# Down of the later groups as seven half-size products in a hybrid decoder step

## The reference, cut to what matters

```python
h = h + (ga * (oa @ w_oa) + gb * (ob @ w_ob)) @ w_out
hn = _rms_norm(h, norm_ffn)
h = h + (jax.nn.silu(hn @ w_gate) * (hn @ w_up)) @ w_down
...
y_prompt = _rms_norm(hp, norm_final)[:, N_META:]
```

## Time and profile before

| | |
|---|---|
| median of 3 runs | 3308.24 us (3306.07 to 3310.15) |
| profiled execution, its own time as the span from first to last instruction | 3313.0 us |
| TensorE busy | 3231.5 us, 98%, 23418 matmuls |
| VectorE, ScalarE, GpSimd busy | 1982.6, 1510.4, 431.1 us |
| moved | 392.45 MB, mean 118 GB/s |

### The profile page before, as it was taken

The page is one execution under the profiler, slowest core; times in us unless marked ns, Lnnn a source line. Parts: engine busy times, 40 slices in busy tenths (PEclk is TensorE's granted clock), DMA queues, the critical chain, the costliest instruction groups (busy, mean ns, idle before and its releaser), DMA issues. The chain is left out here.

```text
span 3313.0 us, 58927 instructions
## 1 busy us (share of the span) xinstructions
PE 3231.5 (98%) x23418; PEld 2825.3 (85%) x23418; DVE 1982.6 (60%) x3740; ACT 1510.4 (46%) x3156; POOL 431.1 (13%) x511
## 2 busy tenths in 40 slices
PE   8999999999999999999999999999999999999998
PEld 7877789999998777898998777889998777789896
DVE  6635545444547654685766754686575855578483
ACT  5434443222234554463554654455454654446362
POOL 2211200432503111000003021000001212000000
PEclk9889999999999999999999999999999999999999
DMA  4211013656643111354553211345463211246462
GB/s 161 65 41 66 28 58 115 230 188 208 248 153 110 54 52 58 119 161 134 170 190 110 73 41 51 110 141 163 140 211 126 75 50 46 77 133 183 124 179 96
DMA packets 142816, 392.45 MB, mean 118 GB/s; under 512 B 18289, under 2 KB 20289, under 8 KB 139073
## 3 DMA queue, kind: packets, MB, share of 16 engines
q1 hardware_dynamic: 142544, 388.69, 36.8%
HBM read 353.95 MB, written 35.69 MB: 118 GB/s over the span
## 5 line engine op out<-in xcount | busy, mean ns | idle before, releaser
L631 DVE TENSOR_TENSOR wl<-raw,wh 128x512 fp32r<-128x512 f32 (+1 forms) x795 | 750.6, 951 | 572.2 <-ACT wh L624 569.4
L624 ACT CAST wh<-raw 128x512 fp32r<-128x512 f32 (+1 forms) x795 | 635.7, 808 | 457.6 <-PE bank L902 374.7
L902 PE MATMUL bank<-xnT,wh 128*128 128x512 f32 (+2 forms) x2432 | 726.2, 382 | 7.3 <-ACT gate L1691 5.8
L902 PE MATMUL bank<-hnT,wh 128*128 128x256 f32 (+2 forms) x3016 | 580.7, 290 | 3.4 <-ACT V L1989 3.4
L902 PEld LDWEIGHTS bank<-xnT,wh 128*128 128x128 f32 x2432 | 430.4, 193 | 80.6 <-issue 16.5
L902 PEld LDWEIGHTS bank<-hnT,wh 128*128 128x128 f32 x3016 | 473.7, 188 | 9.0 <-ACT V L1989 4.2
L902 PE MATMUL bank<-hid,wh 128*128 128x512 f32 (+1 forms) x1760 | 467.5, 353 | 0.0
L902 PE MATMUL bank<-xnT,wl 128*128 128x512 f32 (+2 forms) x1280 | 461.7, 365 | 0.0
L902 PE MATMUL bank<-hnT,wl 128*128 128x256 f32 (+2 forms) x1508 | 437.2, 290 | 0.0
L902 PE MATMUL bank<-Tm,wh 128*128 128x256 f32 x2016 | 368.8, 282 | 0.2
L902 PEld LDWEIGHTS bank<-hid,wh 128*128 128x128 f32 x1760 | 309.5, 188 | 45.8
(11 more groups left out here) (382 smaller groups left out, 4488.3 us busy)
## 6 DMA issues: line engine op xcount, KB each, us to landing
raw<-in_wstream SPq DMA_DIRECT2D x346, 512.0 KB, 3.5
raw<-wsum SPq DMA_DIRECT2D x252, 256.0 KB, 3.4
raw<-in_wstream SPq DMA_DIRECT2D x189, 256.0 KB, 2.8
ops_in<-in_wstream SPq DMA_DIRECT2D x44, 512.0 KB, 7.6
wsum<-ops_out SPq DMA_DIRECT2D x22, 1024.0 KB, 6.3
hT<-in_xT SPq DMA_DIRECT2D x4, 2048.0 KB, 8.9
out_yp_out<-hT SPq DMA_DIRECT2D x16, 512.0 KB, 3.0
xr<-in_x_prompt SPq DMA_DIRECT2D x12, 512.0 KB, 7.2
```

Source lines behind the costliest of these rows:

```text
L624: act.copy(hi_cell(n), raw_cell(n)).then_inc(sem("hi_done"), 1)
L631: nc.vector.tensor_tensor(lo_cell(n), raw_cell(n), hi_cell(n).bitcast(F32), ALU.subtract).then_inc(sem("lo_done"), 1)
L902: ins = nc.tensor.matmul(*a, **k)
```

## The change

The FFN is worked in three chunks of 6, 8 and 8 columns in every group. In group 0 down stays plain, with one unit per output column, and GpSimd makes the four sums for 12 pairs of down's output columns beside the 22 of gate and up. In the later groups down is made of the same seven half-size products: for each pair of output columns (r) all seven, over 3 or 4 block pairs; the units are 384 or 512 columns wide. VectorE adds the banks to `hT` in between, and these adds take the place of copies. The operand sums of hid, their low parts, the sums of squares of down's output and the low parts of the next input are made by GpSimd. The next group's token rows and columns are loaded earlier, in parts, and the rows squared among the products of the last chunk.

```diff
-FFC, FFK = 2, DFF // P // 2
+NFF = DFF // P
+CHUNKS = ((0, 6), (6, 14), (14, NFF))
+DOWN_ORDER = [(r, op) for r in range(NPAIR) for op in OPS]
...
+            def seven_down(c):
+                j0, j1 = CHUNKS[c]
+                m = (j1 - j0) // 2
+                pe.wait_ge(*made("hid_lo", hid_n(j0 + m)))
+                for r, op in DOWN_ORDER:
...
+                    elif op == "S2":
+                        if r == 0:
+                            pe.wait_ge(*made("hid_lo", hid_n(j1) - 1))
+                        pe.wait_ge(*made("h2_done", dn_n(c, r, "A11")))
+                        dn_pass(c, r, op, DX[r], 3)
+                    elif op == "S4":
+                        if r == 0:
+                            pe.wait_ge(*made("hid_lo", hid_n(j1)))
+                        pe.wait_ge(*made("h2_done", dn_n(c, r, "S1")))
+                        dn_pass(c, r, op, DZ[r], 6)
...
             def seven_hid(j):
-                act.wait_ge(*made("hf_done", j + 1))
-                act.copy(hid[0][:, j % FFK, live], hf[j % 2][:, live]).then_inc(sem("hid_hi"), 1)
+                upper, k = place_of(j)
+                act.wait_ge(*made("hid_t", hid_n(j) + 1))
+                if not upper:
+                    act.copy(hidH[k][:, 0:2], hidA32[k][:, 0:2]).then_inc(sem("hid_hi"), 1)
+                    return
+                act.copy(hidH[k][:, 2:4], hidA32[k][:, 2:4]).then_inc(sem("hid_hi"), 1)
+                act.wait_ge(*made("hid_t", hid_n(j) + 2))
+                act.copy(hidH[k][:, 4:7], hidB32[k][:]).then_inc(sem("hid_hi"), 1)
...
+            def hid_sums(j):
+                upper, k = place_of(j)
+                A, B = hidA32[k], hidB32[k]
+                both = lambda ap: ap.broadcast_to([P, 2, HT])
+                tt = nc.gpsimd.tensor_tensor
+                pool.wait_ge(*made("hf_done", j + 1))
+                if not upper:
+                    tt(A[:, 1::2, :], both(A[:, 2:3, :]), both(A[:, 0:1, :]), ALU.subtract).then_inc(sem("hid_t"), 1)
+                    return
+                tt(A[:, 2:4, :], both(B[:, 2:3, :]), A[:, 2:4, :], ALU.subtract).then_inc(sem("hid_t"), 1)
+                pool.wait_ge(*made("hid_t", hid_n(j) + 1))
+                tt(B[:, 0, :], B[:, 1, :], A[:, 3, :], ALU.subtract).then_inc(sem("hid_t"), 1)
+            def hid_rest(j):
...
+                lo = slice(2, 4) if upper else slice(0, 2)
+                tt(hidA[k][:, lo], hidA32[k][:, lo], hidH[k][:, lo].bitcast(F32), ALU.subtract).then_inc(sem("hid_lo"), 1)
+                if upper:
+                    pool.wait_ge(*made("hid_hi", hid_n(j) + 2))
+                    tt(hidB[k][:], hidB32[k][:], hidH[k][:, 4:7].bitcast(F32), ALU.subtract).then_inc(sem("hid_lo"), 1)
...
+                for f in range(KD):
+                    add_square(pool, nc.gpsimd, f - 1, "ysq_done", "yacc_done")
+                    if f >= 4:
+                        for k in (2 * f - 8, 2 * f - 7):
+                            pool.wait_ge(*made("xh_done", k + 1))
+                            nc.gpsimd.tensor_tensor(xnT[1][:, k, MAIN], xT[:, k, :], xnT[0][:, k, MAIN].bitcast(F32),
+                                                    ALU.subtract).then_inc(sem("xl_done"), 1)
+                add_square(pool, nc.gpsimd, KD - 1, "ysq_done", "yacc_done")
...
-            def seven_rest(j):
-                dve.wait_ge(*made("hid_hi", j + 1))
-                v_.tensor_tensor(hid[1][:, j % FFK, live], hf[j % 2][:, live], hid[0][:, j % FFK, live].bitcast(F32), ALU.subtract).then_inc(sem("hid_lo"), 1)
...
+                def add(r, op):
+                    lo_until("dn", len(OPS) * (NPAIR * c + r) + OPS.index(op))
+                    at_, x, cs = plan[op]
+                    dve.wait_ge(*made("down_ps", dn_n(c, r, op)))
...
+                    ins = v_.tensor_tensor(hT[:, 2 * r + x, cs], hT[:, 2 * r + x, cs], bank[at_[r]][:, 0:HT], ALU.add)
+                    ins.then_inc(sem("h2_done"), 1)
```

More of the change, by code:

```diff
@@ L400, in program @@
     hnT = [place(f"hnT{s}", [P, KD, W], F32R, r_gt + s * KD * W * 4) for s in range(2)]
+    hnL = place("hnL", [P, 4, 2, KD // 2, HT], F32R, r_gt)
+    xrL = [place(f"xrL{s}", [P, DM], F32, r_gt + (2 * KD // 2 * HT + s * DM) * 4) for s in range(2)]
     o = r_gt
@@ new lines, in sync @@
+                for c, (j0, j1) in enumerate(CHUNKS):
+                    for j in range(j0, j1):
+                        weights("wu", min(j + 1, j1 - 1))
+                        if j == 0:
+                            sp.wait_ge(*made("out_ps", 2 * KD))
+                        sum_step()
+                        if c and j - j0 in (2, 5):
+                            sum_step()
+                    if c < LASTC:
+                        for f in range(KD):
+                            weights("down", KD * c + f)
+                            if f % 2:
+                                sum_step()
@@ new lines, in sync @@
+                assert summed[0] == NFF + NPAIR * len(CHUNKS)
+                load_until(sp, AHEAD[NUM[(g, "wu", NFF - 1)]])
+                for j in range(summed[0] - 2, summed[0]):
+                    sum_out(j)
+                sp.wait_ge(sem("unit_started"), NUM[(g, "down", KD * LASTC)] + 1)
+                weights("down", KD * LASTC + 2)
+                for t in range(NT):
+                    x_loads(t, xr[t])
+                for q in range(4):
+                    xT_load(q)
+                weights("down", KD * LASTC + KD - 1)
@@ L1522, in h_factors, with operand_pass @@
                 last.then_inc(sem("hR_ps"), 1)
[L1524 to L1528, removed]
+            def operand_pass(w, out, rhs, start, m, ps):
+                w_h, w_l, mm = w
+                for k in range(m):
                     ks = slice(P * k, P * (k + 1))
@@ L1566, in tensor, with x_factors @@
+            def x_factors():
+                claim(6, "xs_done", KD)
+                for t in range(NT):
+                    pe.wait_ge(*made("rr_done", t + 1))
+                    last = spread(t, rr, t, bank[6][:, P * t:P * (t + 1)])
+                last.then_inc(sem("xR_ps"), 1)
+            for cc, (j0, j1) in enumerate(CHUNKS):
+                for j in range(j0, j1):
                     if seven(j):
@@ new lines, in tensor, with hid_ready @@
+                if not first:
+                    seven_down(cc)
+                    continue
+                def hid_ready(k):
+                    pe.wait_ge(*made("hid_hi", j0 + k + 1))
+                    pe.wait_ge(*made("hid_lo", j0 + k + 1))
+                for f in range(KD):
+                    w_h, w_l, mm = unit("down", KD * cc + f)
+                    kh = lambda k: w_h[:, P * k:P * (k + 1)]
+                    kl = lambda k: w_l[:, P * k:P * (k + 1)]
+                    for half in range(2):
+                        b = (2, 5)[f % 2] if half else DB[f % 4]
+                        claim(b, "h2_done", 2 * (KD * cc + f) + half + 1)
+                        last = t_out(mm, bank[b][:, 0:WA], kh, kl, hid[0], hid[1], CB if half else CA, list(range(j1 - j0)),
+                                     ready=hid_ready if f == 0 and half == 0 else None)
+                        last.then_inc(sem("down_ps"), 1)
+                    if cc == LASTC and f == 3 and not last_group:
+                        x_factors()
@@ L2123, in gpsimd @@
             nc.gpsimd.tensor_tensor(hr[:, F:m], hr[:, F:m], nhalf[:, 0:NT], ALU.pow).then_inc(sem("hrr_done"), 1)
-            for j in range(2 * FFK if first else 0):
+            for j in range(NFF + NPAIR * len(CHUNKS) if first else 0):
                 pool.wait_ge(*made("st_in", 32 * (j + 1)))
```

426 lines of the change are left out of this document (272 added, 154 removed).

## The result

The changed kernel takes 3474.8 us (median; 3464.9 to 3481.7) against 3307.6 for the kernel before, a ratio of 1.049 [1.047, 1.052]. It is slower by 167 us. The forecast was 3427 and slower. The median lies 0.2 us inside the outer range (3330 to 3475) and outside the band of 3385 to 3450 that had 0.62; two of the four runs lie above both. The nearest of the courses weighed is the rival of the clock, 3468.

What follows compares the result with a forecast made beforehand. TensorE was taken as the bound, busy 3231.5 of 3313.0 us, VectorE as second limit. Terms -35.6 + 130 + 18 + 3 + 3 = +118 gave 3431 on the span, 3427 us as median; range 3385 to 3450, outer 3330 to 3475.

Steps and rivals of the forecast that it cites:

- the rival of the clock: Chunk-end pauses of 12 to 15 us lower TensorE's clock nine times, 4.6 us each: 3468 us; 0.11 together with another rival.
- Term A: Down of three later groups: 2772 matmuls of 256 columns replace 1584 of 512, gaining 35.6 us if TensorE is fed.
- Rival (4): Down's half-size products run slower than 118 ns, starved by adds or loads: about 3465 us; 0.11 together with the clock rival.
- Term B: GpSimd's hid sums and low parts take turns with VectorE, delaying upper columns and chunk ends: 130 us lost over three groups.
- The cycle of 13.0 us for upper columns: In a chunk's upper half VectorE, GpSimd and ScalarE set each column's pace: 13.0 us instead of 9.93.
- The chain: Upper columns' work up to hid's last pieces before S2: delays of 15.1 us per chunk of 8, 13.2 per chunk of 6.
- Rival (1): Only chain ends count, as splits made ahead absorb the turns: 52 us at chunk ends, 3348 us in all; chance 0.16.
- Term C: Group changes: GpSimd's last twelve operations make TensorE's row sums wait, twice 8.3 us and 1.5 after group 0: 18 us.
- Term D: Group 0's chunk ends: TensorE waits for hid's last low part, 1.2 + 0.4 + 0.4, with GpSimd in the way 3 us.
- Term E: Chunk of 6: raw weight cells turn over in 1.26 us per 1.06 us unit, costing 3 us (0 to 12).
- what I had put at nothing, additions that come late: Down's adds and splits fill 1.11 of 1.42 us: nothing; if 252 adds came 0.1 us late each, 25 us.
- The signs of the prediction: Slower gate/up splits, under 423 matmuls per 50 us in upper halves, gaps before S2, row sums waiting 8 us for GpSimd.

Runs made afterwards that it cites:

- the last version: Changed kernel with hid's sums on VectorE, three pairs ahead of S2, lighter group ends, down's additions before splits, one more piece readied at chunk ends: 3345.9 us.
- experiments 9 and 10: On the 3365.9 us version (hid on VectorE, three pairs ahead, lighter group ends): down's additions before splits, 3350.4 us; then one more down piece readied at chunk ends, 3345.9.
- Experiment 1: Changed kernel with hid's sums and their low parts made by VectorE, none by GpSimd: 3409.2 us.
- experiment 2: Changed kernel with VectorE adding the bank before its next weight splits in down's first two products of a chunk: 3458.0 us.
- experiment 5: Changed kernel with 84 (66 in the last chunk) useless 256-column matmuls ahead of S2's wait at chunk ends of later groups: 3459.0 us.

## Why the prediction was right, and where it was off

**Direction and mechanism held, the size was 48 us short.** Terms on the spans: forecast +118, measured +166.9. That the time still fell into the outer range, by 0.2 us, is luck.

**Term A, fewer columns: right where TensorE is fed.** The starts of 256-column matmuls in down lie 118.8 ns apart, in the mean over all intervals under 130 ns (118.9 in gate and up), against 118.2 in the forecast. Rival (4) is out as to its mechanism: the products themselves are not slower. But "if TensorE is fed" did not hold all through: with the waits' rows taken off, down of the three groups took 368.3 us before and 342.3 in the last version, a gain of 26 and not 35.6, and the short delays named under experiments 9 and 10 are enough to account for it. A stretch of down, where TensorE was busy for 27.21 of 28 us and started 229 matmuls, 118.8 ns each:

```profile
1640.00:1668.00 28.00, 27.21 (x229) 27.00 (x228) 18.99 (x39) 11.67 (x20) 0.00 (x0) 1.00 0.69 209
```

**Term B, GpSimd's work on hid: mechanism right, 113 us instead of 130.** 81.5 us at chunk ends plus 27.8 more on V (31.2 - 3.4) plus 3.9 on the other snapshots. The taking of turns held for the new shapes: splits of 512 columns at a mean of 827 ns in group 1 [687 in rows 6], VectorE's two-input 256-column L2981 at a mean of 649 ns in group 1 (412 in the median of the whole run and up to 2077), while L2982, of the same size and right behind it, never met a GpSimd operation and took 425. By the lock that the Trainium skill ("SBUF — State Buffer", Who interferes with whom) describes this is what must come, and the trace agrees: nowhere do a two-input operation of VectorE and one of GpSimd overlap by more than 0.2 us and both keep their undisturbed length. Experiment 1 tests the cause: moving these operations off GpSimd gives 66 us. The cycle of 13.0 us for upper columns was nearly right: in group 1 the starts of L2987 lie 12.2 to 13.1 us apart there, 12.5 in the mean, against 10.1 in most lower columns (and 10.6 for upper ones in experiment 1). TensorE met part of that delay inside the chunk, 3.6, 3.6 and 4.4 us on snapshots, and the rest at its end, 7.5, 9.8 and 9.8: together 11.1, 13.4 and 14.2 against the forecast 13.2, 15.1 and 15.1. The chain was too long by more than this shows, since the addition of A11 behind a delayed split (experiment 2) is in the measured figures, 2 us at each end, and was missing in the forecast: two errors that partly cancelled. Rival (1) had 52 us for the chunk ends; they alone took 81.5.

**Term C, group changes: right in size, in part by luck.** Square sums waited 11.7 us on GpSimd and 3.6 at the end on VectorE, against 2.7 before, and the next group's first product waited twice 3.05 on the last addition: 18.7 us against the forecast 18. GpSimd cost less than forecast, 4.4 and 6.0 us, not 8.3 each, and a wait that the forecast did not have made up for it: that first product needs bank 0, which the last pair uses; I had not looked at that bank.

**Term D, group 0: 4.2 us against 3.** The waits up to group 1's first wait on a snapshot rose from 47.2 to 52.7 us, of which 1.3 belongs to term C. **Term E, loads of the chunk of 6:** waits on splits are 1.1 us in all, so loads cost next to nothing here, against a forecast 3. In its place stood what I had put at nothing, additions that come late: 10.5 us of waits on down's additions (16.6 less the 6.1 of term C).

**What failed: the clock as a rival.** The forecast held it as another course, at 0.11 together with rival (4), though the condition it named, long pauses at the chunk ends, was part of the forecast itself. It belonged in the sum. Its price, 9 x 4.6 = 41, agrees with the 42.9 us more that were measured behind 1400 us, but by luck: a chunk end cost about 2.1 us of low clock and not 4.6, 19 in all by place and 16 to 18 by experiment 5, and the other 24 stand where the forecast had none, behind the waits for V and at the group changes.

The sum as measured: -35.6 + 113.2 (B) + 18.7 (C) + 4.2 (D) + 10.5 (additions) + 42.9 (clock) = 153.9, and 4.4 more of low clock ahead of 1400 us: 158 of 166.9. The short delays that no row shows, 12 us, are more than the 9 that are missing; the clock sum, which can be somewhat high, may be the other side of it.

**The signs of the prediction.** Splits above 687 ns in gate and up, a gap before S2 with GpSimd as releaser, and row sums waiting for GpSimd (4.4 and 6.0 us, not 8) all showed. TensorE's rate in the upper half of chunks fell too: 370 matmuls in 50 us [423 in rows 2].

```profile
1570.00:1620.00 50.00, 46.13 (x370) 45.43 (x368) 38.44 (x59) 28.47 (x56) 21.73 (x15) 0.97 0.55 154
```

VectorE is busy 38.44 of 50 us there, less than in the earlier trace rows: neither engine looks full, and I take it that the chain through both is what limits; by experiment 1 it shortens when GpSimd is out of it.

## What to carry to other kernels

Moving two-input SBUF work from a busy VectorE to an idle GpSimd can be worse than leaving it, since the two take turns and GpSimd needs about twice as long; count the sum of both engines against the time available, and look at what follows the handover. Where a change brings pauses of some 2 us and more into a TensorE stream at full clock, put the clock into the sum and not among the rivals, and look for every such pause, not only the longest. Before two profiled spans are compared, compare their low clock where the kernels are the same. When a wait is covered by more matmuls ahead of it, check that the supplies those matmuls use up are made in time by the engine that was late.

## What the runs showed of the hardware

- Behind 1400 us of the changed kernel TensorE paused 25 times for 1.8 us or longer. Around 22 of these pauses the granted clock fell to 0.5 (1.2 of 2.4 GHz); around three, of 1.94, 2.19 and 3.07 us, it stayed at 1.00. Before the change the pauses between 1000 us and the last 15 us were of up to 1.7 us, and the clock stayed at 1.00 behind all of them; but in the changed kernel it fell behind one of 1.32 us, at 1003 us. So the length of a pause alone does not decide it. The same pause at the changes of group 1 and group 2 (3.05 us up to 1815.3, 3.07 up to 2644.4) shows both outcomes:

```profile
1818.00:1823.00 5.00, 4.71 (x16) 3.35 (x15) 1.72 (x1) 2.61 (x4) 5.00 (x5) 0.78 0.04 13
2647.00:2652.00 5.00, 3.23 (x14) 2.27 (x13) 1.60 (x1) 2.61 (x4) 5.00 (x5) 1.00 0.08 28
```

- Runs of one kernel differ with the clock: the changed kernel took 3464.9 and 3468.9 us at a mean clock of 0.975 and 0.974, and 3480.7 and 3481.7 at 0.970 and 0.969.
- One blocked operation can be lengthened more than threefold: VectorE's split took 2.30 us for 0.69, beside GpSimd's 768-column operation, which takes 1.80 by itself and 1984 ns in the mean over group 1.
- TensorE kept busy with useless matmuls was faster as a whole: 83 us of added work in place of 81.5 us of waits, 16 us less time.
